# Two operations change places at the end of each feed-forward net, on ScalarE and on VectorE

## The reference

```python
for l in range(DEPTH):                                   # DEPTH = 2
    x = layer_norm(ALPHA * x + 0.5 * swiglu(x, ffn1...), ln1...)
    x = layer_norm(ALPHA * x + hybrid_mixer(x, ...), ln2...)
    x = layer_norm(ALPHA * x + 0.5 * swiglu(x, ffn2...), ln3...)

def swiglu(x, w_gate, w_up, w_down):                     # 1024 -> 2816 -> 1024
    return (silu(x @ w_gate) * (x @ w_up)) @ w_down
```

## Time and profile before

| | us |
|---|---|
| median of 3 executions | 1083.57 (1083.33 to 1083.84) |
| the profiled execution, its time | 1083.67 |
| the profiled execution, its span | 1081.9 |
| TensorE busy | 1072.1 (99%) |
| VectorE busy | 772.0 (71%) |
| ScalarE busy | 579.4 (54%) |

### The profile page before, as it was taken

One profiled execution on the slowest core, in us unless ns is written; L12 is line 12 of the kernel. 1 busy time (PEld: TensorE's weight loads), 2 busy tenths in 40 slices (PEclk: granted clock), 3 DMA queues, 4 the chain that ended last, 5 costly groups with the idle time before them and its releaser, 6 DMA issues.

```text
span 1081.9 us, 14282 instructions
## 1 busy us (share of the span) xinstructions
PE 1072.1 (99%) x5197; PEld 882.7 (82%) x5197; DVE 772.0 (71%) x779; ACT 579.4 (54%) x641; POOL 137.3 (13%) x137
## 2 busy tenths in 40 slices
PE   8999999999999999999999999999999999999997
PEld 6888888888888788888888888888878887888886
DVE  5756557799979775555679665677999787655566
ACT  5755654768554544444456655547774546344441
POOL 1498000000000000000006970000000000000000
PEclk9999999999999999999999999999999999999999
DMA  8877879355566486777737877775455674688761
GB/s 285 263 216 231 296 223 225 105 184 171 175 185 208 149 272 226 233 259 225 250 124 231 248 244 254 230 199 165 148 166 157 195 268 133 209 268 270 235 208 40
DMA packets 192371, 226.39 MB, mean 209 GB/s; under 512 B 31540, under 2 KB 157128, under 8 KB 192328
## 3 DMA queue, kind: packets, MB, share of 16 engines
q1 hardware_dynamic: 192328, 225.83, 65.5%
HBM read 214.26 MB, written 11.53 MB: 209 GB/s over the span
## 4 chain that ended last, share of the span: by engine, by line
PE 97%; DMA 1%; SPq 1%; DVE 1%; issue 0%; ACT 0%; DVEq 0%
PE ps L578 25%; PE ps L555 19%; PE ps L557 18%; PE ps L556 18%; PE ps L538 4%; PE ps L540 2%; PE ps L974 1%; PE ps L976 1%; PE ps L975 1%; PE ps L593 1%; DMA raw<-in_ffn_w_up 1%; PE ps L901 1%; DMA tp<-in_ln_b 0%; PE ps L686 0%; PE ps L685 0%; PE ps L684 0%
## 5 line engine op out<-in xcount | busy, mean ns | idle before, releaser
L1449 DVE TENSOR_TENSOR w_lo<-raw,w_hi 128x2048 fp32r<-128x2048 f32 x172 | 399.9, 2329 | 166.7 <-ACT w_hi L1058 165.6
L1058 ACT CAST w_hi<-raw 128x2048 fp32r<-128x2048 f32 x172 | 328.1, 1910 | 162.1 <-PE ps L578 78.9
L555 PE MATMUL ps<-w_hi,xT 128*128 128x512 f32 x848 | 331.8, 391 | 0.3 <-DVE w_lo L1461 0.2
L556 PE MATMUL ps<-w_lo,xT 128*128 128x512 f32 x848 | 330.1, 389 | 0.0
L557 PE MATMUL ps<-w_hi,xT 128*128 128x512 f32 x848 | 330.1, 389 | 0.0
L555 PEld LDWEIGHTS ps<-w_hi,xT 128*128 128x128 f32 x848 | 159.2, 188 | 36.2 <-issue 2.5
L557 PEld LDWEIGHTS ps<-w_hi,xT 128*128 128x128 f32 x848 | 159.2, 188 | 33.0
L556 PEld LDWEIGHTS ps<-w_lo,xT 128*128 128x128 f32 x848 | 159.2, 188 | 32.7
L578 PE MATMUL ps<-w_hi,rows_hi 128*128 128x512 f32 x396 | 126.6, 393 | 0.0
L578 PE MATMUL ps<-w_hi,rows_lo 128*128 128x512 f32 x396 | 125.4, 390 | 0.0
L578 PE MATMUL ps<-w_lo,rows_hi 128*128 128x512 f32 x396 | 125.2, 389 | 0.0
(11 more groups left out here) (248 smaller groups left out, 1117.1 us busy)
## 6 DMA issues: line engine op xcount, KB each, us to landing
raw<-in_ffn_w_down SPq DMA_DIRECT2D x44, 1024.0 KB, 6.6
raw<-in_ffn_w_gate SPq DMA_DIRECT2D x86, 512.0 KB, 4.1
raw<-in_ffn_w_up SPq DMA_DIRECT2D x86, 512.0 KB, 5.2
raw<-in_w_in SPq DMA_DIRECT2D x30, 1024.0 KB, 5.1
hid_dram<-qT SPq DMA_DIRECT2D x160, 64.0 KB, 2.8
qT<-hid_dram SPq DMA_DIRECT2D x40, 256.0 KB, 2.6
raw<-in_w_out SPq DMA_DIRECT2D x8, 1024.0 KB, 4.9
raw<-in_w_in SPq DMA_DIRECT2D x8, 512.0 KB, 5.0
```

Source lines behind the costliest of these rows:

```text
L555: mm(o, xT[:, c, 0, tok], h, start=c == UPPER_FIRST[0], stop=False, skip_group_check=True)
L556: mm(o, xT[:, c, 0, tok], w, start=False, stop=False, skip_group_check=True)
L1058: nc.scalar.copy(w_hi[s][:, :], raw[s][:, :]).then_inc(hi_made.sem, 1)
L1449: tt(w_lo[s][:, :], raw[s][:, :], f32(w_hi[s][:, :]), ALU.subtract).then_inc(lo_made.sem, 1)
```

## The change

On ScalarE the high part of the last down chunk is put ahead of the high part of the last turned values that come through DRAM. On VectorE the first tile product of the last step is put ahead of the low part of that chunk. Nothing is added or removed.

```diff
@@ scalar block, ffn @@
                     split_tenth(k0 + FFN_CHUNKS - 2)
                 else:
                     split(l, k0 + FFN_CHUNKS - 2)
+                split(l, k0 + FFN_CHUNKS - 1)
                 hidden_hi(l, b0 + STEPS - 1, final)
-                split(l, k0 + FFN_CHUNKS - 1)
                 silu(l, s0 + STEPS, (half_used.sem, half_used.at(l, f + 1)), 4, slice(0, 1))
                 if following:
                     split_first(*following)
@@ vector block, ffn @@
                 else:
                     rest(l, k0 + FFN_CHUNKS - 2)
                 hidden_lo(l, s0 + STEPS - 1, final)
+                hidden(l, s0 + STEPS, 4, slice(0, 1))
                 rest(l, k0 + FFN_CHUNKS - 1)
-                hidden(l, s0 + STEPS, 4, slice(0, 1))
```

## The result

The changed kernel takes 1085.97 us (median of 18 executions), the kernel before 1083.7 us on the same chips (18 executions): ratio 1.0018, 95% interval 1.0011 to 1.0024. That is 2.27 us more by the medians, and 1.95 (1.19 to 2.60) by the ratio; it is clear of noise. The forecast was 1085.8.

What follows compares the result with a forecast made beforehand. TensorE, 99% busy, was taken to bound the kernel, with VectorE's queue the last link at net ends. 3 x 0.74 = 2.2 us on the profiled 1083.67 gave 1085.9, or 1085.8 by the median; range 1084.2 to 1086.6.

Steps and rivals of the forecast that it cites:

- Only TensorE's waits count, and the ends' last link is VectorE's queue.: Ends of nets: TensorE 99% busy; VectorE's queue, not TensorE's sums, sets the residual and so the load at L593.
- 0.74 at each of three ends.: Ends of nets one to three, VectorE: 0.53 later start + 0.61 subtraction formerly in idle time - 0.40 pause = 0.74 us.
- upper bound per end: First three ends: at most 0.95 us each, if three waits newly meeting the queue each lose their 0.08 overlap.
- The product sooner gains nothing.: First tile product ready at 176.87, over one us sooner; its transposes still load at 178.34, so no gain.
- The last net is free.: End of the last net: the second product waits for its silu anyway; cost nothing, cover 0.07 us at worst.
- The wait at L578 about 0.7.: First three ends, TensorE: a new weight-load wait of about 0.7 us at L578, for VectorE's L1505.
- Strictly in order.: Skill rule: ScalarE and VectorE take instructions strictly in order; without it the time would stay at 1083.6.
- Absorbed: Rival, chance 0.15: TensorE still gets the normalised tile in time; no change, 1083.6 to 1084.7.
- Late loads: Rival: SyncE issues the next chunk 1.47 us later; three places 4.4 us, 1088.0. Chance 0.05, shared with another further wait.
- A gain at L740: Rival, chance 0.03: first product's transposes load sooner, 0.34 us per end, 1.0 over three ends, 1082.5.
- Nothing gives the time back.: Behind the late transposes ScalarE and VectorE wait for them and move along; TensorE has no slack later.

Runs made afterwards that it cites:

- the tight place: Kernel before plus one unread 128x512 VectorE subtraction at the first three ends, behind the next chunk's low part, where the queue has no pause: 1085.97 us, ratio 1.0019.
- the deferred half: Changed kernel with the second half of the second next chunk's low part moved behind the normalise of tile 0 at three ends: 1084.2 us against 1084.29 before.
- both with half a chunk deferred: Changed kernel and kernel before, each with half of the second next chunk's low part moved behind the normalise of tile 0: 1084.2 and 1083.67 us.

## Why the prediction was right

*Only TensorE's waits count, and the ends' last link is VectorE's queue.* Right: the same 0.6 us cost 0.60 in the queue and nothing ahead of it. The reading that VectorE's queue and not TensorE's sums sets the residual was true by little: with slack in the queue the residual came only 0.12 sooner (7.31 in place of 7.43). So what makes the queue later costs in full, and what makes it shorter gains next to nothing; the prediction did not see the second.

*0.74 at each of three ends.* ScalarE, then VectorE, timeline, nets two and three; first the kernel before, then the changed one:

```profile
527.10 0.38 ACT L1079 ACTIVATE act<-ps 128x256 f32<-128x256 f32 x1 [0.76 <-PE ps L557]
709.80 0.38 ACT L1079 ACTIVATE act<-ps 128x256 f32<-128x256 f32 x1 [0.76 <-PE ps L557]
```

```profile
528.65 0.39 ACT L1079 ACTIVATE act<-ps 128x256 f32<-128x256 f32 x1 [0.23 <-PE ps L557]
712.10 0.39 ACT L1079 ACTIVATE act<-ps 128x256 f32<-128x256 f32 x1 [0.23 <-PE ps L557]
...
536.81 0.69 DVE L1571 SCALAR_TENSOR_TENSOR xtok<-xtok,ps 128x512 f32<-128x512 f32 x1
720.26 0.69 DVE L1571 SCALAR_TENSOR_TENSOR xtok<-xtok,ps 128x512 f32<-128x512 f32 x1
```

At nets two and three the residual lies at 536.81 - 528.65 = 8.16 and 720.26 - 712.10 = 8.16 behind the silu, where it was 7.43 (527.10 and 709.80 to the earlier trace rows). So 0.73 three times, 2.19 in all, against 2.27 by the medians. The terms hold: the turned values' low part starts 0.20 ahead of the silu (176.64 against 176.84), where the sum had 175.85 against 176.04; the long subtraction starts 1.48 later than before, by the silu as zero (0.76 against -0.72), for which I had 1.47; the pause of 0.32 ahead of the next chunk is gone. By its own terms the prediction's upper bound per end is 0.74 + 3 x 0.08 = 0.98 and not 0.95; nothing hangs on it.

*The product sooner gains nothing.* It is ready 0.84 after the silu, in place of 1.90, and L740 is loaded at 179.14 - 176.84 = 2.30 behind the silu, as before.

*The last net is free.* Right, and with more cover than the 0.07 that I had as the worst: 0.19, because the cast there starts 0.12 sooner against the silu (1056.66 to 1059.33, before 1055.55 to 1058.10).

*The wait at L578 about 0.7.* The load waits 0.85, and L593 moves by 0.73. The difference stood in the kernel before already, too short to be shown as a wait:

```profile
186.58 0.41 PEld L578 LDWEIGHTS ps<-w_hi,rows_lo 128*128 128x128 f32 x2
187.11 0.19 PEld L578 LDWEIGHTS ps<-w_hi,rows_hi 128*128 128x128 f32 x1
```

There the load stands 187.11 - (186.58 + 0.41) = 0.12 behind the one ahead of it, so 0.73 of the 0.85 is new.

*Strictly in order.* No row of the kernel before showed a VectorE instruction that was ready behind one that waited. The changed kernel's does: the last chunk's cast ends at 176.09, VectorE stands idle until 176.64, and the subtraction that was ready starts at 177.60 behind two others. The rule of the Trainium skill (Perfetto Trace Analysis, Tensor Engine Instruction) that ScalarE and VectorE are strictly in order holds here for VectorE.

*The rivals.* Absorbed: refuted by the wait at L578 and by the tight place. Late loads: refuted by the deferred half. A gain at L740: the load did not move.

*Nothing gives the time back.* Nearly. By the silus the profiled execution fell behind the one of before by 0.75, 0.75 and 0.55 from each end to the next, 2.05 in all: 0.2 us of the 2.2 came back behind the third end, in the second mixer, where TensorE's pace differed (below). The prediction had no term for this. Whether it comes with the change is open: the profiles of the two kernels with one half of the change have the quicker pace too, that of the kernel with the tight place, which is 0.60 late at the ends, has not.

## What to carry to other kernels

On an engine that works in order, do not move an instruction that waits ahead of a long one that is ready: the long one's lateness goes through the whole queue. VectorE's half of this change did just that, and ScalarE's half did the same by making the instruction ahead of the long one wait. Before a move, look for the last pause ahead of the instruction that the bottleneck waits for; the same operation cost 0.60 us behind it and nothing ahead of it. When starts of executions differ, measure from an event that the bottleneck itself releases (here the silu), which showed 0.73 us three times where the total time needed 18 executions.

## What was not expected of the hardware

The executions of one kernel spread by 2 to 3 us (1085.14 to 1087.0 and 1082.86 to 1085.57), as much as the effect, and the profiles show one source: in the first steps of a net the turned values come back from DRAM late in some executions. ScalarE, timeline, one of these waits in the kernel with the tight place:

```profile
81.44 0.62 ACT L1090 CAST rows_hi<-qT 128x512 fp32r<-128x512 f32 x1 [8.17 <-DMA qT<-hid_dram]
```

and in the kernel before:

```profile
77.70 0.62 ACT L1090 CAST rows_hi<-qT 128x512 fp32r<-128x512 f32 x1 [5.82 <-DMA qT<-hid_dram]
```

By the silus of the steps that execution was 2.85 us behind the one of before when it came to its first changed instruction. The profile of the changed kernel with half a chunk deferred, the slowest of its eleven executions (1086.31), lost 1.1 us early in net three, where such a wait is 7.43 in place of 5.79. Why the transfers are late there is open.

TensorE's pace is not one number even where it waits for nothing and the granted clock is 1.00: in the second mixer a pair of L538 and L540 follows the last after 0.353 us in the kernel before (30 pairs from 744.14 to 754.74) and after 0.347 in the changed one (30 pairs from 747.15 to 757.55). Over these 30 pairs this is the 0.2 us that came back. Of the nine kernels' profiles, three have 0.347 over these pairs: the changed kernel and the two with one half of it, the ones that are 0.7 us late at the ends. The other six, the tight place and both with half a chunk deferred among them, have 0.353 or 0.354. With one profile of each kernel this is no proof of a link, and what sets the pace was not tried.
